# One mixed order for two attentions and twenty input tiles in a one-core decoder step

## The chip, the core and the metric

The kernel runs on one core of one Trainium2 chip. The metric is the device time of one execution, in microseconds (us). Its engines are TensorE (PE: matmuls and transposes), VectorE (DVE), ScalarE (ACT), GpSimd (POOL) and SyncE (SP, which here issues most DMAs). Each engine works through its own instructions in the order in which the program lists them; semaphores tie the engines together.

## The reference, cut to what matters

One decoder layer for a prompt group (512 tokens) and a sample group (8 sequences of 4 new tokens, each with 1024 cached positions in pages of 128). All is float32.

```python
z = rmsnorm(x, norm_mix_w) @ w_in        # 1024 -> gb, gc, u (512 each) and q, k, v (4 heads x 128)
yconv = gb * causal_dwconv(gc * u)        # conv mixer, width 3
s  = (q[c] . k[c]) * 64**-0.5 + rel_bias  # two score maps per head, c = 0, 1
a  = softmax(s[0]) - lam * softmax(s[1])
o  = rmsnorm(a @ v) * subln_w * 0.8       # per head; samples read k, v of 8 pages and the new ones
x += concat[yconv, o] @ w_out
x += cross_attention(rmsnorm(x), memory)  # 4 heads, 256 memory tokens
x += conv_ffn(rmsnorm(x))                 # 1024 -> 2 x 2816 -> 1024
```

## The kernel before

**Tiles.** Activations lie transposed, channels on the partitions, 544 columns: two halves of 256 prompt and 16 sample tokens. A projection is cut into tiles of 128 output channels. Each fp32 product is made from three fp32r ones: a weight tile `w_raw` is split into `w_hi` (`split_hi`, ACT, L1221) and `w_lo` (`split_lo`, DVE, L1518), and an activation into `a_hi` and `a_lo`. `tile(n)` (L936) does, for each of 8 blocks of 128 rows, w_hi by a_hi, w_hi by a_lo and w_lo by a_hi on both halves: 48 matmuls of 272 columns into the two banks of `proj[n % 2]`. DVE then takes the 544 columns out (`tile` on DVE, L1647, L1666), scaled by `rstd`. Tiles alternate between `proj[0]` and `proj[1]`.

**Order.** `make_schedule()` writes one list of steps. Each engine's program walks that list and emits its own part of a step, so the list is the order on every engine. The part that matters begins after the q tiles. Twenty tiles are left of the input projection: k0 to k3, v0 to v3, then gb, gc, u for each of four channel groups. Twelve of them each stand whole ahead of a portion of the samples' attention (`plan`). The other eight are spread in halves (`half_tile`, then `tile`) over the prompt's attention (`ticks`).

**Samples.** For each of two groups of four sequences and each pair of pages: `k_turn` transposes 8 pages' keys head by head through the banks T0 (copied out by ACT) and T1 (copied out by DVE), and `k_score` multiplies them with `q_rows` into S0. `s_soft` is a softmax over 1056 positions (DVE maximum, ACT exp, DVE scale). `s_turn` transposes the probabilities, `s_pv` (L1053) multiplies them with pages of values into S1, `s_new` adds the new tokens, `s_norm` normalizes (ACT squares, two table loads, scaled copies), `s_out` transposes into `b_hi` and `b_lo`. SP loads the pages, 8 at a time, into a ring of 16 (`load_self`); its eight register loads come before each group's eight DMAs.

**Prompt.** Sixteen units (four query blocks i by four heads h); unit u = 4i + h sees i + 1 key blocks. `p_score`: matmuls into S0 and S1 (L1079); DVE adds the bias (L1776, L1780) and takes the maximum (L1785); ACT takes exp, which frees S0 and S1 (L1382). `p_mix`: DVE forms p0/z0 - lam p1/z1 (L1799 to L1803). `p_turn`: transposes through T0, ACT copies to `p_keys` (L1390). `p_pv` (L1098): with the values into T1, 128 columns a head. After four heads `p_norm` (ACT, L1396 and the tables of L1226 and L1227), `p_scale` (DVE, T1 to `o_blk`), `p_out` (transposes, then ACT `b_hi`, DVE `b_lo`). A tick u of the old order is `p_mix(u-1)`, `p_out`, `p_score(u)`, `p_scale`, a half tile, `p_turn(u-1)`, `p_pv(u-2)`, `p_norm`.

**Mixer.** `conv(c)` (DVE, L1674 to L1535) follows the u tile; `mix(c)` (DVE, L1688 to L1690) multiplies with the gate and writes `b_hi` and `b_lo`.

The stage ends with the first tile of the output projection (`out add 0`), which needs all of `b_hi` and `b_lo`.

Of the kernel before, what the change touches and what calls it, by code (L numbers as in the profile page):

```python
# [17 lines left out]
F32 = mybir.dt.float32  # L18
# [6 lines left out]
P = 128  # L25
# [15 lines left out]
DIST = 384  # L41
# [55 lines left out]
def make_tiles():  # L97
# [36 lines left out]

def make_schedule():
# [18 lines left out]

    fill = [("in", "k", h) for h in range(HEADS)] + [("in", "v", h) for h in range(HEADS)]
    fill += [("in", kind, c) for c in range(CT) for kind in ("gb", "gc", "u")]
    after = {("in", "k", h): [("k_out", h)] for h in range(HEADS)}
    after |= {("in", "v", h): [("v_out", h)] for h in range(HEADS)}

    def turns(g, kq, hp, behind=None):  # L160


        steps = []
        for j in range(2):
            steps.append(("k_turn", g, kq, hp, j))
            if behind:
                steps.append(("k_score", g, *behind, j))
        return steps

    def keys(g, kq):  # L170
        return turns(g, kq, 0, (kq - 1, 1) if kq else None) + turns(g, kq, 1, (kq, 0))

    def scores(g, kq, hp):
        return [("k_score", g, kq, hp, j) for j in range(2)]


    plan = [keys(0, kq) for kq in range(4)]
    plan.append(scores(0, 3, 1) + turns(1, 0, 0) + turns(1, 0, 1) + [("s_soft", 0)])
    plan.append([("s_turn", 0)] + scores(1, 0, 0) + [("s_pv", 0, 0)])
    plan.append([("s_pv", 0, 1)] + keys(1, 1))  # L180
    plan.append([("s_pv", 0, 2)] + keys(1, 2))
    plan.append([("s_pv", 0, 3), ("s_new", 0)] + keys(1, 3) + [("s_norm", 0)])
    plan.append(scores(1, 3, 1) + [("s_soft", 1)])
    plan.append([("s_turn", 1), ("s_pv", 1, 0), ("s_pv", 1, 1)])
    plan.append([("s_pv", 1, 2), ("s_out", 0), ("s_pv", 1, 3), ("s_new", 1), ("s_norm", 1)])
    units = [(i, h) for i in range(SEQ // P) for h in range(HEADS)]

    half_at, fill_at = range(3, 17, 2), range(4, 18, 2)
    ticks = []
    for u in range(len(units) + 4):  # L190
        tick = []
        if 0 <= u - 1 < len(units):
            tick.append(("p_mix", *units[u - 1]))
        if u >= 4 and units[u - 4][1] == HEADS - 1:
            tick.append(("p_out", units[u - 4][0]))
        if u < len(units):
            tick.append(("p_score", *units[u]))
        if 3 <= u < len(units) + 3 and units[u - 3][1] == HEADS - 1:
            tick.append(("p_scale", units[u - 3][0]))
        if u in half_at:  # L200
            tick.append("half")
        if u in fill_at:
            tick.append("fill")
        if 0 <= u - 1 < len(units):
            tick.append(("p_turn", *units[u - 1]))
        if 0 <= u - 2 < len(units):
            tick.append(("p_pv", *units[u - 2]))
            if units[u - 2][1] == HEADS - 1:
                tick.append(("p_norm", units[u - 2][0]))
        ticks += tick  # L210
    assert len(plan) + len(fill_at) + 1 == len(fill)
    late = []
    for part in plan:
        f = fill.pop(0)
        tile(*f)
        if f[1] == "u":
            part = part + [("conv", f[2]), ("mix", f[2])]
        if ("s_new", 0) in part:
            part = late + part
        else:  # L220
            at = len(part) - 1 if part[-1][0] == "k_score" else 0
            part = part[:at] + late + part[at:]
        late = list(after.get(f, []))
        s.extend(part)
    ticks.insert(0, "fill")
    for n, step in enumerate(ticks):
        if n == 3:
            s.append(("s_out", 1))
        if step == ("p_pv", 3, 3):
            s.append(("mem_in",))  # L230
        if step == ("p_out", 3):
            s += [("half_tile", TILE["out", "add", 0]), step]
            s += [("squares", k, "mem") for k in range(KT)]
            continue
        if step == "half":
            s.append(("half_tile", TILE[fill[0]]))
            continue
        if step == "fill":
            f = fill.pop(0)
            tile(*f)  # L240
            if f[1] == "u":
                late += [("conv", f[2]), ("mix", f[2])]
            continue
        s.append(step)
        if step[0] == "p_score":
            s.extend(late[:1])
            late = late[1:]
        if step == ("p_turn", 3, 3):
            s.extend(late)
# [82 lines left out]

def number_fills():

    count = dict(S0=0, S1=0, T0=0, T1=0)
    out, held = [], {}

    def use(slot):
# [3 lines left out]
    for step in SCHEDULE:  # L342
        kind = step[0]
        uses = [use(slot) for slot in FILLS.get(kind, [])]
        if kind == "k_score":
            if step[3:] == (0, 0):
                held["k"] = use("S0")
# [1580 lines left out]
```

## Time and profile before

| what | value |
| --- | --- |
| median of 3 runs | 1054.36 us (1051.03 to 1056.3) |
| span of the profiled execution | 1050.4 us |
| TensorE busy | 973.8 us, 93% of the span |
| VectorE busy, ScalarE busy | 573.0 us (55%), 388.4 us (37%) |
| mean granted TensorE clock | 0.974 |
| the twenty tiles and both attentions, to the end of `out add 0` | 49.0 to 345.3 us, 296.3 us |

The profiled execution is one execution with its own time: for it the record has the span, from its first to its last instruction. That lies 4.0 us (0.4%) below the median of the three timed runs and 0.6 us below the lowest of them. Durations below are those of this one execution. A step can be found in the trace by its line. In the timelines the end of a matmul is modelled and overlaps the next one, so the time that a group takes is read from its start to the start of the next. An fp32 matmul with a separate moving operand (L1025, L1053, L1079, L1098) stands in the trace as two records; a transpose (L948) and an fp32r matmul (L936) as one.

### The profile page before, as it was taken

To read this page: it belongs to the slowest core of one execution; us is meant where nothing else is said; L and a number is where in the kernel's file an instruction comes from. 1 tells how busy PE (TensorE), PEld (TensorE's weight loads), DVE (VectorE), ACT (ScalarE), POOL (GpSimd) and SP (SyncE) were. 2 spreads that over 40 slices of the span, in tenths; PEclk is the share of its full clock that TensorE was granted. 3 is DMA by queue.
4 is the path that set the end of the run, shared out by engine and by line. 5 is a ranking of instruction groups with operands and counts; after the bars stand their busy time and mean duration, and the time that the engine had idled before them with its cause. 6 is when DMAs were issued, how large, how long until landed. Compare 5 with 4: busy or idle time off the path is not lost.

```text
span 1050.4 us, 19193 instructions
## 1 busy us (share of the span) xinstructions
PE 973.8 (93%) x7675; PEld 887.6 (85%) x7675; DVE 573.0 (55%) x997; ACT 388.4 (37%) x691; POOL 97.9 (9%) x213
## 2 busy tenths in 40 slices
PE   5999989977887999999888999999999999999995
PEld 5977766746777999998755999999999999999994
DVE  4544423627687646335433447778347783477542
ACT  5422212234436547224422335433124331243343
POOL 2211000000000011100000002222002220122000
PEclk8999998998999999999989999999999999999998
DMA  8656678831101245634562322323323223332213
GB/s 251 194 173 218 202 248 279 270 121 41 41 21 41 83 124 154 229 118 141 190 251 80 95 81 82 100 81 90 92 81 100 82 84 91 88 97 80 71 37 100
DMA packets 162492, 131.36 MB, mean 125 GB/s; under 512 B 5820, under 2 KB 139223, under 8 KB 162371
## 3 DMA queue, kind: packets, MB, share of 16 engines
q1 hardware_dynamic: 159940, 124.40, 38.4%
q0 software_dynamic: 2320, 5.68, 1.8%
q8 instruction: 61, 1.00, 0.4%
q14 instruction: 27, 0.21, 0.1%
q10 hardware_dynamic: 144, 0.07, 0.0%
HBM read 123.12 MB, written 7.00 MB: 124 GB/s over the span
## 4 chain that ended last, share of the span: by engine, by line
PE 78%; DVE 8%; ACT 6%; issue 4%; SPq 2%; DMA 2%; DVEq 0%; ACTq 0%
PE proj L936 63%; PE T L948 7%; PE score L1025 2%; PE score L1141 1%; PE score L1126 1%; PE score L1053 1%; ACT pages L1382 1%; DVE small L1785 1%; ACT w_hi L1221 1%; DVE score L1780 1%; DMA w_raw<-in_w_in 1%; SPq L659 1%; PE score L1159 1%; SPq L676 1%; DVE a_lo L1584 1%
## 5 line engine op out<-in xcount | busy, mean ns | idle before, releaser
L936 PE MATMUL proj<-a_hi,w_hi 128*128 128x272 f32 (+1 forms) x992 | 222.7, 296 | 4.8 <-DVE a_lo L1584 2.7
L936 PE MATMUL proj<-a_hi,w_lo 128*128 128x272 f32 (+1 forms) x992 | 216.9, 290 | 0.0
L936 PE MATMUL proj<-a_lo,w_hi 128*128 128x272 f32 (+1 forms) x992 | 216.8, 290 | 0.0
L1221 ACT ACTIVATE w_hi<-w_raw 128x1024 fp32r<-128x1024 f32 (+1 forms) x132 | 137.0, 1038 | 155.6 <-PE proj L936 144.6
L1518 DVE TENSOR_TENSOR w_lo<-w_raw,w_hi 128x1024 fp32r<-128x1024 f32 (+1 forms) x132 | 159.0, 1205 | 61.1 <-ACT w_hi L1221 60.7
L936 PEld LDWEIGHTS proj<-a_hi,w_hi 128*128 128x128 f32 x992 | 162.2, 191 | 16.1 <-issue 13.4
L936 PEld LDWEIGHTS proj<-a_lo,w_hi 128*128 128x128 f32 x992 | 162.5, 192 | 0.1
L936 PEld LDWEIGHTS proj<-a_hi,w_lo 128*128 128x128 f32 x992 | 161.5, 192 | 0.0
L936 PE MATMUL proj<-d_hi,w_hi 128*128 128x272 f32 x704 | 145.5, 288 | 0.0
L936 PE MATMUL proj<-d_hi,w_lo 128*128 128x272 f32 x704 | 144.8, 288 | 0.0
L936 PE MATMUL proj<-d_lo,w_hi 128*128 128x272 f32 x704 | 144.6, 287 | 0.0
L936 PEld LDWEIGHTS proj<-d_lo,w_hi 128*128 128x128 f32 x704 | 110.0, 188 | 0.0
L936 PEld LDWEIGHTS proj<-d_hi,w_hi 128*128 128x128 f32 x704 | 109.7, 188 | 0.2
L936 PEld LDWEIGHTS proj<-d_hi,w_lo 128*128 128x128 f32 x704 | 109.6, 189 | 0.0
L1625 DVE TENSOR_TENSOR x<-proj,x 128x544 f32<-128x544 f32 x40 | 29.0, 724 | 109.6 <-PE proj L936 109.6
L1474 ACT ACTIVATE conv<-up_pad,fvec 128x512 f32<-128x512 f32 x44 | 36.0, 818 | 134.8 <-DVE up_pad_s L1658 134.8
L890 POOL COPY f_state<-up_pad 128x2 f32<-128x2 f32 x44 | 47.4, 1077 | 306.6 <-DVE up_pad_s L1658 306.6
L1656 DVE TENSOR_TENSOR up_pad<-proj,rstd 128x512 f32<-128x512 f32 x44 | 30.4, 691 | 55.1 <-PE proj L936 47.8
L948 PE MATMUL T<-ident,pages 128*128 128x128 f32 x248 | 40.8, 304 | 13.4 <-DMA pages<-in_x_prompt 5.7
L948 PEld LDWEIGHTS T<-ident,pages 128*128 128x128 f32 x248 | 30.5, 154 | 26.3 <-issue 9.8
L1348 ACT ACTIVATE turned<-T 128x512 f32<-128x512 f32 x32 | 19.1, 597 | 79.0 <-PE T L948 79.0
L1703 DVE COPY turned<-T 128x512 f32<-128x512 f32 x32 | 22.1, 691 | 33.3 <-PE T L948 32.8
(257 smaller groups left out, 1262.9 us busy)
## 6 DMA issues: line engine op xcount, KB each, us to landing
w_raw<-in_w_up SPq DMA_DIRECT2D x44, 512.0 KB, 3.8
w_raw<-in_w_in SPq DMA_DIRECT2D x24, 512.0 KB, 4.8
pages<-in_cache_k SPq DMA_DIRECT2D x40, 256.0 KB, 4.4
early_pages<-in_cache_v SPq DMA_DIRECT2D x40, 256.0 KB, 4.7
w_raw<-in_w_ckv SPq DMA_DIRECT2D x16, 512.0 KB, 4.0
c_pages<-in_cache_mem_k SPq DMA_DIRECT2D x16, 512.0 KB, 6.4
c_pages<-in_cache_mem_v SPq DMA_DIRECT2D x16, 512.0 KB, 5.3
w_raw<-in_w_down SPq DMA_DIRECT2D x16, 448.0 KB, 3.7
```

Source lines behind the costliest of these rows:

```text
L659: physical.append(sp.value_load(page_ids[0:1, slot:slot + 1], min_val=0, max_val=src.shape[1] - 1))
L890: pool.tensor_copy(f_state[:, j * FT + i, 0:2], up_pad[:, j, i % 2, SEQ:SEQ + 2]).then_inc(sem("f_state_ready"), 1)
L936: mm = pe.matmul(proj[n % 2][:, half, 0:width], wt, act[:, k, half * HALF:half * HALF + width], start=(k == 0 and a == 0), stop=(k == w["k ...
L948: mm = pe.transpose(bank[use[0]][0:width, col:col + rows], src, ident[0:rows, 0:rows])
L1025: mm = pe.matmul(bank["S0"][32 * b:32 * b + 32, 0:2 * P], q_rows[:, h, GB * g + b, :], k_turned[:, half % 2, b, h2 * 2 * P:(h2 + 1) * 2 * ...
L1221: act.activation(w_hi[:, n % W_HI_RING, 0:kt, :], w_raw[:, n % W_RING, 0:kt, :], ACT.Copy).then_inc(w_hi_ready, 1)
L1348: act.activation(k_turned[:, half % 2, 2 * step[4], :], bank["T0"], ACT.Copy).then_inc(free["T0"], 1)
L1474: act.activation(prompt(conv[:, j, :]), by_half(up_pad[:, j, i % 2, 0:SEQ]), ACT.Identity, bias=bias, scale=w0).then_inc(sem("first_tap"), 1)
L1518: dve.tensor_tensor(w_lo[:, n % W_RING, 0:kt, :], w_raw[:, n % W_RING, 0:kt, :], w_hi[:, n % W_HI_RING, 0:kt, :].bitcast(F32), ALU.subtrac ...
L1625: dve.tensor_tensor(halves(x[:, w["i"], :]), out[:, :, 0:HALF], halves(x[:, w["i"], :]), ALU.add).then_inc(tile_out[arg % 2], 1)
L1656: dve.tensor_tensor(by_half(up_pad[:, j, i % 2, 2:2 + SEQ]), prompt_of(out), prompt(rstd), ALU.mult).then_inc(sem("up_in"), 1)
L1703: dve.tensor_copy(k_turned[:, half % 2, 2 * step[4] + 1, :], bank["T1"]).then_inc(free["T1"], 1)
```

## The change

The two attentions no longer follow one another. `mixed_periods()` makes twenty periods, one for each tile. In each, the samples' own events and up to two prompt ticks (`TICKS`) are merged in proportion, and the tile is cut into 16 pieces of three matmuls (first half 0, all 8 blocks, then half 1), which are dealt out between the events. All twenty tiles use `proj[0]` alone; each half is evicted by DVE by itself (`half_out`). The two banks of `proj[1]` become `N` (samples' scores) and `H` (samples' values). A prompt unit's `p_pv` uses T1 alone, and ACT copies it to `o_blocks` and squares it at once. `k_turn` handles one head of four sequences; the exp of a unit is a step of its own (`p_exp`); `p_scale` now stands ahead of `p_mix` and `p_score` in its tick. `split(n + 2)` stands at the head of period n. The order of the mixer's tiles becomes gc, u, gb, `conv` is cut in three parts that stand in the gb period, and `mix` at the head of the next.

```diff
-        for j, kind in enumerate(("gb", "gc", "u")):
+        for j, kind in ((1, "gc"), (2, "u"), (0, "gb")):
...
+AFTER_FILL = {("in", "k", h): [("k_out", h)] for h in range(HEADS)}
+AFTER_FILL |= {("in", "v", h): [("v_out", h)] for h in range(HEADS)}
+AFTER_FILL |= {("in", "gb", c): [("mix", c)] for c in range(CT)}
+TICKS = {7: [0], 8: [1], 9: [2, 3], 10: [4, 5], 11: [6, 7], 12: [8], 13: [9, 10], 14: [11], 15: [12], 16: [13],
+         17: [14], 18: [15], 19: [16]}
+def prompt_events(u):
...
+    first = [("p_scale", (u - 3) // HEADS)] if ends(u - 3) else []
+    if 0 <= u - 1 < PROMPT_UNITS:
+        first.append(("p_mix", *unit(u - 1)))
+    if u < PROMPT_UNITS:
+        first.append(("p_score", *unit(u)))
+    events = [first]
+    if u < PROMPT_UNITS:
+        events.append([("p_exp", *unit(u))])
+    if ends(u - 3) and (u - 3) // HEADS >= 2:
+        events.append([("p_out", (u - 3) // HEADS)])
+    if 0 <= u - 2 < PROMPT_UNITS:
+        events.append([("p_pv", *unit(u - 2))])
+    if 0 <= u - 1 < PROMPT_UNITS:
+        events.append([("p_turn", *unit(u - 1))])
+    if ends(u - 2):
+        events.append([("p_norm", (u - 2) // HEADS)])
...
+    samples.append(values(1, 3) + [[("s_new", 1)], [("p_out", 0)], [("s_out", 0)]])
+    samples.append(norm(1)[:3] + [[("p_out", 1)]] + norm(1)[3:])
+    samples.append([[("s_out", 1)]])
+    samples.append([])
...
+    for fill, events in zip(FILL_TILES, mixed_periods()):
+        n = TILE[fill]
+        s.append(("split", n + 2))
+        s += AFTER_FILL.get(FILL_TILES[FILL_TILES.index(fill) - 1], []) if n > FIRST_FILL else []
+        for j, event in enumerate(events):
+            for piece in range(PIECES * j // len(events), PIECES * (j + 1) // len(events)):
+                s.append(("piece", n, piece))
+                if piece == KT - 1:
+                    s.append(("half_out", n))
+                if piece == PIECES - 1:
+                    tile(*fill)
+            s += event
+    s += AFTER_FILL[FILL_TILES[-1]]
+    s.append(("mem_in",))
+    s += prompt_tick(PROMPT_UNITS + 1)
+    s.append(("half_tile", TILE["out", "add", 0]))
+    s += prompt_tick(PROMPT_UNITS + 2)
...
-                if (kind == "k_turn" and step[3:] == (0, 0)) or kind == "s_pv":
+                if (kind == "k_turn" and step[3] == HEADS - 1) or (kind == "s_pv" and step[3] == 1):
                     if self_loads:
                         load_self(*self_loads.pop(0))
...
+            def piece(n, part):
+                half, k = divmod(part, KT)
...
+                if k == 0 and n > FIRST_FILL:
+                    pe.wait_ge(half_out, 2 * (n - 1 - FIRST_FILL) + half + 1)
...
+                pe.matmul(out, w_h, a_hi[:, k, cols], start=(k == 0), stop=False)
+                pe.matmul(out, w_h, a_lo[:, k, cols], start=False, stop=False)
+                mm = pe.matmul(out, w_l, a_hi[:, k, cols], start=False, stop=(k == KT - 1))
+                if k == KT - 1:
+                    mm.then_inc(half_done if half == 0 else tile_done, 1)
...
+                elif kind == "p_pv":
+                    h = step[2]
+                    cols = slice(h * P, (h + 1) * P)
+                    wait_full(act, uses[0])
+                    o = o_blocks[step[1]][:, cols]
+                    act.activation(o, bank["T1"][:, 0:P], ACT.Copy).then_inc(free["T1"], 1)
+                    wait_taken(act, *uses[0])
+                    act.activation(o_sq[:, :], o, ACT.Square,
+                                   accum_out=small[:, 28 + h:29 + h]).then_inc(sem("o_squared"), 1)
```

## Rows read from the trace of the kernel before

**Rows 1.** Stretches of the span: busy us (instructions) per engine, granted clock, DMA share, GB/s.

```profile
49.00:101.70 52.70, 51.18 (x449) 41.63 (x448) 23.43 (x33) 14.45 (x24) 6.68 (x20) 1.00 0.59 187
...
227.50:345.30 117.80, 95.01 (x638) 82.92 (x638) 88.05 (x202) 56.67 (x155) 0.00 (x0) 0.91 0.13 37
49.00:345.30 296.30, 262.09 (x1997) 208.93 (x1997) 158.94 (x324) 103.63 (x243) 10.63 (x26) 0.95 0.47 149
```

**Rows 2.** TensorE's waits from 49 to 345.3 us: total us, times, longest.

```profile
PE score L1079 <- ACT pages L1382: 10.6, 8, 3.1
PE T L1098 <- DVE pages L1790: 4.8, 3, 3.4
...
PE T L948 <- DMA pages<-in_cache_k: 1.9, 1, 1.9
```

**Rows 3.** TensorE timeline, keys after a tile: start, us, instruction.

```profile
94.31 1.04 PE L948 MATMUL T<-ident,pages 128*128 128x128 f32 x8
95.28 0.64 PE L1025 MATMUL score<-turned,q_rows 128*32 128x256 f32 x8
95.85 1.09 PE L948 MATMUL T<-ident,pages 128*128 128x128 f32 x8
```

**Rows 4.** TensorE timeline, values of pages and one prompt unit.

```profile
134.36 1.92 PE L1053 MATMUL score<-early_pages,norm_area 128*32 128x512 f32 x16
...
299.06 0.49 PE L948 MATMUL T<-ident,pages 128*128 128x128 f32 x3
299.38 0.83 PE L1098 MATMUL T<-v_tok,pages 128*128 128x128 f32 x6
302.27 2.40 PE L1079 MATMUL score<-k_t,q_t 64*128 64x256 f32 x8 [2.05 <-ACT pages L1382]
```

**Rows 5.** Windows on a whole tile and two half tiles: busy us, granted clock.

```profile
88.20:94.31 6.11, 6.11 (x52) 6.11 (x49) 1.35 (x2) 0.75 (x1) 1.32 (x2) 1.00 0.93 289
...
304.60:308.66 4.06, 4.06 (x25) 4.06 (x25) 3.92 (x9) 0.00 (x0) 0.00 (x0) 0.74 0.00 0
...
312.48:315.59 3.11, 3.11 (x26) 3.11 (x25) 3.08 (x5) 3.06 (x7) 0.00 (x0) 1.00 0.02 5
```

**Rows 6.** VectorE timeline: mix, split, eviction, then p_mix and p_score of a unit.

```profile
301.32 0.71 DVE L1688 TENSOR_TENSOR norm_area<-norm_area 128x544 f32<-128x544 f32 x1
...
302.55 0.72 DVE L1690 TENSOR_TENSOR b_lo<-norm_area,b_hi 128x544 fp32r<-128x544 f32 x1
303.86 1.23 DVE L1518 TENSOR_TENSOR w_lo<-w_raw,w_hi 128x1024 fp32r<-128x1024 f32 x1 [0.59 <-ACT w_hi L1221]
305.00 0.72 DVE L1647 TENSOR_TENSOR norm_area<-proj,rstd 128x544 f32<-128x544 f32 x1
305.64 0.15 DVE L1799 RECIPROCAL small<-small 128x2 f32<-128x2 f32 x1
...
307.21 0.75 DVE L1776 TENSOR_SCALAR score<-score,near 128x512 f32<-128x512 f32 x1
...
308.66 1.22 DVE L1785 TENSOR_REDUCE small<-score 128x2 f32<-128x1024 f32 x1
```

**Rows 7.** ScalarE timeline: p_exp, p_turn, then the two table loads of p_norm.

```profile
309.92 0.69 ACT L1382 ACTIVATE pages<-score,small 128x512 f32<-128x512 f32 x1 [5.71 <-DVE small L1785]
...
311.26 0.59 ACT L1390 ACTIVATE pages<-T 128x512 f32<-128x512 f32 x1
...
312.90 1.28 ACT L1226 ACT_TABLE_LOAD   x1
...
315.81 0.20 ACT L1227 ACTIVATE small<-small 128x4 f32<-128x4 f32 x1
```

**Rows 8.** VectorE group from 227.5 to 345.3 us: busy, mean ns, idle before.

```profile
L1518 DVE TENSOR_TENSOR w_lo<-w_raw,w_hi 128x1024 fp32r<-128x1024 f32 x9 | 11.0, 1223 | 10.4 <-ACT w_hi L1221 10.4
```

**Rows 9.** VectorE timeline, first and last operation of one conv step.

```profile
293.48 0.68 DVE L1674 TENSOR_TENSOR pre<-pre,rstd 128x512 f32<-128x512 f32 x1
...
297.07 0.24 DVE L1535 SCALAR_TENSOR_TENSOR norm_area<-pre_s,vec,norm_area 128x32 f32<-128x32 f32 x1
```

More of the change, by code:

```diff
@@ new lines @@
+TICKS = {7: [0], 8: [1], 9: [2, 3], 10: [4, 5], 11: [6, 7], 12: [8], 13: [9, 10], 14: [11], 15: [12], 16: [13],
+         17: [14], 18: [15], 19: [16]}
+def prompt_events(u):
+    unit = lambda n: divmod(n, HEADS)
+    ends = lambda n: 0 <= n < PROMPT_UNITS and n % HEADS == HEADS - 1
+    first = [("p_scale", (u - 3) // HEADS)] if ends(u - 3) else []
[14 more added lines that the diff above has]
+        events.append([("p_norm", (u - 2) // HEADS)])
+    return [e for e in events if e]
@@ L153, in make_schedule @@
     s += [("near",), ("q_blocks",)]
[L155 to L249, printed above, removed]
+    for fill, events in zip(FILL_TILES, mixed_periods()):
[10 more added lines that the diff above has]
+            s += event
@@ L359, in number_fills @@
             uses = [held["s", step[1]]]
-        if kind == "p_pv":
-            if step[2] == 0:
-                held["p", step[1]] = use("T1")
-            uses = [held["p", step[1]]]
-        if kind in ("p_norm", "p_scale"):
-            uses = [held["p", step[1]]]
         if kind == "ck_score":
@@ L388 @@
 PAGE_GROUPS = [(step[1], "k" if step[0] == "k_turn" else "v", step[2]) for step in SCHEDULE
-               if (step[0] == "k_turn" and step[3:] == (0, 0)) or step[0] == "s_pv"]
+               if (step[0] == "k_turn" and step[3] == 0) or (step[0] == "s_pv" and step[3] == 0)]
 def self_page(g, cache, kq, b, pg):
@@ L632, in build @@
         LATE_NORMS = ["mem"]
+        AFTER_IN = TILE["out", "add", 0]
         use_of = {step: uses for step, uses, _ in NUMBERED}
@@ L1013, in _ @@
                         turn(uses[j], parts)
                 elif kind == "k_score":
[L1015 to L1016 removed]
+                    g, kq, h = step[1:]
+                    if h == 0:
                         pe.wait_ge(sem("q_rows_ready"), 2 * HEADS)
                         wait_empty(pe, uses[0])
[L1019 to L1022 removed]
@@ L1042, in _ @@
                 elif kind == "s_pv":
[L1043 to L1044 removed]
+                    g, kq, pg = step[1:]
+                    if kq == 0 and pg == 0:
                         wait_empty(pe, uses[0])
```

404 lines of the change are left out of this document (239 added, 165 removed), and 2 rows, old and new, of the table FILLS.

## The prediction

> **What bounds the kernel now.** I read the stretches of the span first. The change lies between 49.0 us (start of tile k0) and 345.3 us (end of `out add 0`), 296.3 us; what comes before and after is not touched. In that stage TensorE is busy for 262.1 us and idle for 34.2, at a mean granted clock of 0.95. The first stretch is dense (51.2 busy of 52.7, clock 1.00); the last, where the prompt's attention runs, is not (95.0 of 117.8, clock 0.91, VectorE busy for 88.1) [rows 1]. The list of waits says for whom: 10.6 us of p_score for the exp that frees S0 and S1, 4.8 us of p_pv for p_scale, 1.9 us in one wait for late pages [rows 2].
>
> How much of the stage is TensorE's own work? A tile takes 6.11 us and there are twenty and `out add 0`: 128. Eight transposes of a k_turn take 0.97 (94.31 to 95.28), a k_score 0.57 (95.28 to 95.85), 32 of each: 49 [rows 3]. The values of one group of pages take 1.92, eight of them 15 [rows 4]. A prompt unit with three key blocks takes 0.32 for p_turn and 0.83 for p_pv [rows 4], and about 0.9 for the scores, an estimate, since the one shown ran partly at the low clock; over sixteen units with one to four blocks that is 26. The other transposes (k_out, v_out, s_turn, p_out, mem_in and the rest) are some 130 at 0.12: 16, with s_new 2. Sum 236. So before, waits and slow clock hold 60 us, and that is all that a new order can give back. If the pieces hid every one, the time would fall by 5.7%. The question is how many it puts in their place.
>
> **What the order adds on TensorE.** A whole tile behind a k_score took 6.11 and a half tile 3.11 [rows 5]. Two equations, 48m + r and 24m + r, give m = 0.125 a matmul and r = 0.11 for the return from small matmuls to the tile. There are 80 events with small matmuls (32 k_score, 16 s_pv, 16 p_score, 16 p_pv), each now followed by a piece; before some 28 such returns: 52 x 0.11 = 6. Three matmuls in succession into one bank instead of two banks in turn: not in these rows; bounds 0 and, if every one of 960 cost 0.01 more, 10. I take 0, as it is the same number of columns.
>
> **What it removes.** Late pages: a period with keys is 13 to 15 us and one with values about 10, and a page group is now asked for at the last read of its slots, two groups ahead; I count the wait of 1.9 us as gone. Waits of the samples' steps for copies mostly go, since a piece of 0.375 us stands between.
>
> **What it adds: a split at the head of each period.** `split(n + 2)` stands ahead of everything else of a period: ACT 1.05 [rows 7], then DVE 1.23 [rows 6], so DVE is free 2.3 us into the period at the earliest, and 0.7 later has copied k_out or v_out out of T0. The first k_turn is ready for T0 after k_out (0.64) and two pieces (0.75): it waits 1.05 us in four periods, 1.4 in that of gc0, and about 2 more go to s_turn and T1 in two others. Queued behind are all pieces. Waits of the first ten periods: 7; they come to 130 us.
>
> **The chain through DVE and ACT.** For a unit with four key blocks p_mix is 1.6 us (305.64 to 307.21) and p_score 2.7 (307.21 to 309.88) on DVE [rows 6], then exp 1.4 on ACT (309.92 to 311.3) [rows 7]; for one block I take 1.1, 0.9 and 0.8. A conv is 3.8 (293.48 to 297.31) [rows 9], a mix 1.95 (301.32 to 303.27), two half evictions 0.44 each (one of all columns is 0.72 [rows 6]; bounds 0.36 and 0.72). p_norm on ACT is 3.1 (312.90 to 316.01) [rows 7]. DVE already stood for 10.4 us ahead of nine splits, waiting for ACT's half [rows 8]. I followed the new list step by step from period 10 (gb0), counting from each period's start:
> - gb0 has 19 events for 16 pieces. DVE: split, copy, conv, mix, score of unit 4 to 9.9, and so on to 14.8. TensorE waits 2.3; 16.9 long.
> - gc1: ACT has p_norm(0) ahead of its split, so w_hi comes at 3.4, w_lo at 4.6, then mix 6.5, scores of samples 7.2, p_scale 7.9, p_mix(5) 9.1. p_turn(5) was ready at 6.7. Waits 2.9; 17.0 long.
> - u1: s_turn's third fill of T0 waits for DVE, which has the split, p_mix(7) and p_score(8) first (5.9): 3.3 of waits; 12.4 long.
> - gb1: conv on DVE ahead of unit 8's mix; then p_norm(1) runs on ACT from 14.4 to 17.5, and p_scale(1) now stands ahead of p_mix(9) and p_score(10) on DVE. p_turn(9), ready at 16.3, goes at 19.7. Waits 7.7; 20.0 long.
> - gc2 and u2: what DVE is late holds back the eviction of a half: 2.2; 22.6 long.
> - gb2: p_out(0) fills T0; `b_hi` stands behind exp(13) on ACT, `b_lo` behind p_score(13) and its exp: T0 is free at 14.25 and p_turn(12) was ready at 10.0. 4.3; 16.6 long.
> - gc3: p_norm(2) delays the split to 5.0; mix, p_scale: p_out(2) goes at 7.7 instead of 4.0. Then p_out(1) needs T0, whose `b_hi` stands behind exp(14) (13.3) and s_norm's tables (16.4) on ACT: from 9.0 to 17.9 TensorE stands. 12.7; 21.9 long.
> - u3 and gb3: 3.1, the last p_turn behind the conv; 19.1 long.
> - Behind the last period: mem_in, p_pv(15), p_norm, p_scale, p_out, `out add 0`: 12.9 with 3.5 of waits.
>
> Waits of these: 42; with the first ten 49. A dip of the clock has cost a half tile 0.95 us (4.06 for 3.11, at a mean of 0.74 [rows 5]); four of the waits are over 3 us, so 4.
>
> **Sum.** 236 + 6 + 49 + 4 = 295 us for a stage of 296.3: the span goes from 1050.4 to 1049, and the median of the runs, 4.0 above the profiled execution, from 1054.4 to 1053. The waits of which the kernel is rid and those that it gets are about equal. The two orders have the same weakness, 3.1 us of tables ahead of a split or an exp; the new one adds p_scale ahead of p_score and three p_out behind them.
>
> ScalarE's tables decide much of this, and here row and skill differ. Each load took 1.28 and the next instruction began 0.02 later [rows 7]. The Trainium skill (ScalarE: Activation LUTs, "What ACT_TABLE_LOAD costs") gives 1283 ns for the load too, and about 1380 ns of drain with it, 2.66 us in all. By the page a p_norm would be 5.8 us, and six norms would give up to 16 us more, a time of 1069; by the row it is 3.1. I go by the row.
>
> **Rivals.**
> (A) The forecast: 1053, of itself 1043 to 1064. Chance 0.40.
> (B) The pieces hide more: every late step of DVE starts the next ones late too, and I may have counted one delay in two periods; also where TensorE runs ahead, later waits shrink. If half of the 49 us go, and two dips with them, the stage is 268: 1026. For it speaks that DVE needs only 159 of 296 us in the stage [rows 1]; against it, that the waits are for order and not for throughput, as the 10.4 us ahead of the splits show. Chance 0.30.
> (C) Slower, by the clock. TensorE works some 93 of 127 us in the eight periods gb0 to gc3, with stands of 1 to 9 us all through, where the last stretch before has a clock of 0.91 [rows 1]. At a mean of 0.75 the 93 us become 124, at 0.91 they are 102: 22 more, a time of 1075. It decides from about 0.86 on (108, 6 more). Against it: the first ten periods have short stands alone, and the first stretch before, with such, has 1.00 [rows 1]. The Trainium skill (TensorE: Matmul & The Clock Gate, "A second HAM failure mode: psum-queue depth-cycling") tells of a kernel whose many small idles between groups of matmuls made the clock swing; by it the dense ten periods would suffer as well. Chance 0.20.
> (D) Pages late. A group and a tile's weights are 2.6 MB in a period; the periods with values are 10 us, 260 GB/s, where the first stretch moved 187 at a share of 0.59 [rows 1]. Two us in each of six periods: 1065. Against it, twice the rate is not needed for long. Chance 0.10.
>
> **How the numbers follow.** About 0.5% (5.3 us) is what a measurement of this kernel can tell from no change. A lies under 1049.1 with a third of its chance, over 1059.6 with a tenth: 0.13, 0.23, 0.04. B is faster but for 0.01; C slower, 0.20; D half same and half slower. Faster 0.42, same 0.29, slower 0.29. The range is 1019 to 1075: it takes in B with 7 us below its time, since the share of the waits that goes may be more than half, and ends at C's; about 0.08 is left below and 0.10 above. The bounds of the unknown costs (return 0 to 0.11 each, bank 0 to 10, eviction 0.36 to 0.72, which is 0 to 6 over the periods in which DVE is late) lie inside.
>
> **What would show it.** Right: in gc3 TensorE stands for about 9 us ahead of the transposes of p_out(1), released by DVE's `b_lo`; in gb1 about 3.4 ahead of p_turn(9), DVE idle ahead of p_scale for some 5 us; in gb2 some 4 ahead of p_turn(12); about 1 ahead of the first k_turn in k1 to k3; no wait for pages over 1 us. The ten first periods end near 179 us, the stage near 344. Wrong: a stage under 280 with these stands short (B); a clock under 0.86 from gb0 to gc3 (C); waits of L948 or L1053 for DMA (D). What I may have mis-sized is above all the propagation of lateness between the three queues, as every entry above hangs on the one before it.

## The result and the profile after

| | us |
|---|---|
| kernel before, median of 4 runs | 1053.6 (1051.0 to 1056.3) |
| kernel after, median of 4 runs | 1064.7 (1063.7 to 1066.0) |
| ratio after / before | 1.011, 95% interval 1.009 to 1.013 |
| predicted | 1053.0, range 1019 to 1075 |

Forecast was no change; the kernel is 1.1% slower. The page of the profile after begins so (span; then busy time, share of the span and instructions of each engine):

```profile
span 1063.1 us, 19216 instructions
PE 975.9 (92%) x7675; PEld 891.3 (84%) x7675; DVE 575.2 (54%) x1021; ACT 394.9 (37%) x707; POOL 98.0 (9%) x213
```

The stage runs from 49.06 to 355.78 us, 306.7 long where before had 296.3 [rows 1]: 10.4 of the span's 12.7 us. The rest of the difference (2.2 us) lies behind the stage, where nothing was changed; in the profiles of the fifteen kernels below, none of which touches that part, it took 703.5 to 707.5 us, in part by how much low clock it had. So a difference of 2 to 4 us between two profiled executions can lie there. The stretches of after, in the columns of [rows 1]:

```profile
49.06:355.78 306.72, 262.96 (x1996) 211.70 (x1995) 160.55 (x347) 109.90 (x259) 10.62 (x26) 0.93 0.45 143
49.06:101.00 51.94, 46.09 (x390) 38.00 (x389) 21.23 (x33) 13.40 (x21) 8.00 (x22) 0.97 0.54 166
...
297.95:321.08 23.13, 12.70 (x77) 11.66 (x77) 10.15 (x19) 11.63 (x28) 0.00 (x0) 0.69 0.08 23
305.30:318.95 13.65, 5.57 (x27) 5.28 (x26) 5.80 (x11) 5.91 (x11) 0.00 (x0) 0.50 0.00 0
56.15:59.55 3.40, 3.40 (x20) 2.70 (x13) 0.44 (x1) 0.00 (x0) 0.00 (x0) 0.50 0.00 0
...
250.70:257.55 6.85, 6.58 (x28) 5.63 (x27) 2.43 (x7) 4.19 (x10) 0.00 (x0) 0.50 0.22 82
...
188.16:321.08 132.92, 106.50 (x725) 82.51 (x723) 79.40 (x184) 55.69 (x146) 0.00 (x0) 0.87 0.35 110
```

Such rows split a stage in three. TensorE's idle time is length less busy. Low clock is the stretches at 0.50, the lower of the two levels (1.2 GHz); half of the busy time in them is counted as lost against the full clock, which is an estimate. What is left is work at the full clock. After has nine such stretches in the stage, three of which stand above, with 44.6 us and 35.4 busy; before has five, with 27.5 and 23.9 (its stage ends 0.2 us earlier here than in [rows 1]).

| stage, us | length | idle | lost to low clock | work at full clock |
|---|---|---|---|---|
| before | 296.1 | 34.2 | 12.0 | 249.9 |
| after | 306.7 | 43.8 | 17.7 | 245.2 |
| predicted for after | 295 | 49 | 4 | 242 |

So the mixed order did save 4.7 us of work, and paid 9.6 of idle time and 5.7 of clock. TensorE's waits, called stands below, in the stage (total, times, longest), where [rows 2] were those of before:

```profile
PE T L991 <- DVE b_lo L1831: 11.2, 2, 8.1
PE T L991 <- DVE p_exp L1867: 4.8, 4, 2.5
PE T L991 <- DVE turned L1855: 4.0, 2, 2.3
PE T L991 <- DVE norm_area L1801: 3.8, 2, 3.3
PE T L991 <- ACT o_blk L1441: 3.5, 1, 3.5
PE T L991 <- DVE v_tok L1762: 3.4, 2, 2.7
PE T L991 <- DVE norm_area L1759: 3.3, 3, 1.1
PE proj L1066 <- POOL q_rows L853: 2.1, 1, 2.1
```

The 10.6 us for S0 and S1 have become 1.5 and the wait for pages is gone. In their place nearly every wait is one of a transpose (L991) for a bank or an operand: a short instruction of VectorE or ScalarE that stands behind another step in its queue. The timeline shows three places.

```profile
65.81 1.23 DVE L1563 TENSOR_TENSOR w_lo<-w_raw,w_hi 128x1024 fp32r<-128x1024 f32 x1 [0.71 <-ACT w_hi L1258]
...
66.95 0.69 DVE L1759 COPY norm_area<-T 128x512 f32<-128x512 f32 x1
...
67.78 1.06 PE L991 MATMUL T<-ident,pages 128*128 128x128 f32 x8 [1.11 <-DVE norm_area L1759]
...
194.05 0.60 PE L991 MATMUL T<-ident,early_pages 128*128 128x128 f32 x4
198.19 0.66 PE L991 MATMUL T<-ident,early_pages 128*128 128x128 f32 x4 [3.54 <-ACT o_blk L1441]
...
196.95 0.47 ACT L1427 ACTIVATE p_exp<-score,small 128x256 f32<-128x256 f32 x1 [6.35 <-DVE small L1850]
...
309.16 0.69 ACT L1427 ACTIVATE p_exp<-score,small 128x512 f32<-128x512 f32 x1 [6.55 <-DVE small L1850]
...
310.62 1.28 ACT L1263 ACT_TABLE_LOAD   x1
...
312.23 1.28 ACT L1264 ACT_TABLE_LOAD   x1
...
313.63 0.67 ACT L1420 ACTIVATE b_hi<-T,sub_w 128x512 fp32r<-128x512 f32 x1
...
314.40 0.75 DVE L1831 SCALAR_TENSOR_TENSOR b_lo<-T,sub_w,b_hi 128x512 fp32r<-128x512 f32 x1 [4.87 <-ACT b_hi L1420]
...
315.30 1.09 PE L991 MATMUL T<-ident,turned 128*128 128x128 f32 x4 [8.08 <-DVE b_lo L1831]
```

First, k1: `split` ahead of the copy of k_out; TensorE stands for 1.11 us. Second, gb0: k_turn needs T1, which holds p_pv(2), whose copy is behind exp(4) on ScalarE, which waited for VectorE's maximum. Third, gc3: p_out(2) has filled T0; its `b_hi` on ScalarE is behind exp(14) and the two table loads of the samples' norm; p_out(1) stands for 8.1 us, from 307.2 to 315.3, and a low clock of 13.65 us lies around it: it begins at 305.3, 1.9 us ahead of the stand and behind an earlier one of 2.3 us, and ends 3.7 us behind it.

### The profile page after: what moved, and what is told of

Read it like the earlier page. It is cut to its first block, busy times and chain, and to the rows that moved or that the text cites. A ratio compares the mean times of both kernels' runs of the same rounds, so it can differ in the third digit from the quotient of the medians.

```text
span 1063.1 us, 19216 instructions
## 1 busy us (share of the span) xinstructions
PE 975.9 (92%) x7675; PEld 891.3 (84%) x7675; DVE 575.2 (54%) x1021; ACT 394.9 (37%) x707; POOL 98.0 (9%) x213
## 4 chain that ended last, share of the span: by engine, by line
PE 76%; DVE 9%; ACT 6%; issue 4%; SPq 2%; DMA 1%; POOL 0%; DVEq 0%; ACTq 0%; POOLq 0%
PE proj L961 56%; PE T L991 7%; PE proj L979 3%; PE proj L981 2%; PE proj L980 2%; PE score L1178 1%; ACT w_hi L1258 1%; DMA w_raw<-in_w_in 1%; PE proj L1066 1%; PE score L1163 1%; DVE w_lo L1563 1%; ACT p_exp L1427 1%; DVE small L1850 1%; SPq L681 1%; SPq L698 1%
## 5 line engine op out<-in xcount | busy, mean ns | idle before, releaser
L961 PE MATMUL proj<-a_hi,w_hi 128*128 128x272 f32 (+1 forms) x672 | 152.8, 294 | 4.7 <-DVE a_lo L1629 2.6
L961 PE MATMUL proj<-a_hi,w_lo 128*128 128x272 f32 (+1 forms) x672 | 150.0, 290 | 0.0
L961 PE MATMUL proj<-a_lo,w_hi 128*128 128x272 f32 (+1 forms) x672 | 149.8, 289 | 0.0
L961 PEld LDWEIGHTS proj<-a_hi,w_hi 128*128 128x128 f32 x672 | 111.6, 192 | 6.7 <-issue 4.4
L961 PEld LDWEIGHTS proj<-a_lo,w_hi 128*128 128x128 f32 x672 | 111.2, 191 | 0.1
L961 PEld LDWEIGHTS proj<-a_hi,w_lo 128*128 128x128 f32 x672 | 110.5, 191 | 0.0
L979 PE MATMUL proj<-a_hi,w_hi 128*128 128x272 f32 x320 | 108.1, 338 | 1.1 <-DVE norm_area L1691 1.1
L981 PE MATMUL proj<-a_hi,w_lo 128*128 128x272 f32 x320 | 95.3, 298 | 0.0
L980 PE MATMUL proj<-a_lo,w_hi 128*128 128x272 f32 x320 | 95.2, 298 | 0.0
L979 PEld LDWEIGHTS proj<-a_hi,w_hi 128*128 128x128 f32 x320 | 63.4, 198 | 29.1 <-issue 24.8
L980 PEld LDWEIGHTS proj<-a_lo,w_hi 128*128 128x128 f32 x320 | 63.8, 199 | 0.0
```

The source lines that it names most:

```text
L961: mm = pe.matmul(proj[n % 2][:, half, 0:width], wt, act[:, k, half * HALF:half * HALF + width], start=(k == 0 and a == 0), stop=(k == w["k ...
L979: pe.matmul(out, w_h, a_hi[:, k, cols], start=(k == 0), stop=False)
L980: pe.matmul(out, w_h, a_lo[:, k, cols], start=False, stop=False)
L981: mm = pe.matmul(out, w_l, a_hi[:, k, cols], start=False, stop=(k == KT - 1))
```

## The experiments

T1: the stands come from what lies ahead of short copies in the queues of VectorE and ScalarE, so moving a step regains them. T2: the cut into pieces costs by itself. T3: the stands bring the low clock, which about doubles what they cost. In each diff, minus is the kernel after, unless the text says otherwise. Ratios are to the kernel before, timed beside each kernel; the kernel after has 1.0111. The kernels were timed in groups, and the kernel before had medians from 1052.2 to 1054.1 us in them, so a difference of medians from two groups can be off by up to 2 us; 0.001 of the ratio is 1.05 us. How idle time and clock share a gain is read from one execution of each kernel.

### Two blocks of eight pieces

```diff
-            for piece in range(PIECES * j // len(events), PIECES * (j + 1) // len(events)):
+            block = {0: range(KT), len(events) // 2: range(KT, PIECES)}.get(j, ())
+            for piece in block:
```

> The kernel after, but each tile's sixteen pieces stand in two blocks of eight, one ahead of a period's first event and one at its middle; events, their order and all work are the same. Theory T1 (waits placed by the order on the queues of VectorE and ScalarE set the time, and the cut itself costs nothing): the events of a half period stand with no pieces between them, so their chains are bare again, 10 us or more slower than the kernel after (1075 or more). Theory T2 (the cut into three-matmul pieces, with its changes of bank and weights, costs): about 100 returns fewer, at 0.05 to 0.1 us each 5 to 10 us faster (1055 to 1060). Theory T3 (the clock): the longer stands bring more low clock, another 5 us slower.

1057.7 us, ratio 1.0041 (1.0024 to 1.0058): 7 us faster than after. T1's number was wrong, and wrong in sign. The stretches say why (the stage, k1 to k3, gb3):

```profile
49.31:348.69 299.38, 256.47 (x1997) 208.96 (x1995) 160.13 (x347) 108.91 (x259) 10.62 (x26) 0.93 0.46 147
63.61:102.58 38.97, 38.97 (x355) 31.98 (x352) 17.60 (x27) 10.81 (x19) 3.98 (x6) 1.00 0.67 225
321.39:327.65 6.26, 6.26 (x53) 6.26 (x52) 3.09 (x10) 3.45 (x9) 0.00 (x0) 1.00 0.29 86
```

Work at the full clock is 241.4 us (256.5 less half of 30.2 busy at the low clock), 3.8 less than after: that is T2's part, measured. And k1 to k3 have no wait at all, as eight pieces, 3 us, cover the split. The idle time of the stage is hardly less all the same, 42.9 us for 43.8: gb1 stands for 5.5 us and not 2.4, v0 for 2.5 and not 1.0. In gb3 the sixteen pieces stand together and take 6.10 us from start to start, as much as the whole tile of before in two banks (6.11). So this run could not tell the cut from the split's place; a later one does (below).

### The split behind the second event

```diff
-        s.append(("split", n + 2))
...
             s += event
+            if j == min(1, len(events) - 1):
+                s.append(("split", n + 2))
```

> The kernel after, but the split of the tile after next stands behind the second event of a period, not ahead of all, on every engine that takes part. T1: the 1.1 us stands of TensorE in three keys periods and the 2.7 us in the period of the first gc tile (VectorE still in the split when its copy out of the bank is due) go: 4 to 6 us faster, 1059 to 1061. Rival: the split is then late for the tile that needs it or moves the same wait one event on: within 1.5 us of the kernel after.

1043.4 us, ratio 0.9914 (0.990 to 0.9928): 21 us faster than after and faster than before, by one step moved. It was put at 4 to 6. Stretches (stage, k1 to k3, gc3) and the longest waits:

```profile
49.18:336.17 286.99, 256.63 (x1996) 207.51 (x1995) 161.67 (x348) 109.39 (x259) 10.54 (x26) 0.95 0.49 153
65.69:105.67 39.98, 39.93 (x355) 32.47 (x352) 17.87 (x27) 10.82 (x18) 3.99 (x6) 1.00 0.70 216
...
283.23:303.21 19.98, 12.63 (x78) 11.81 (x77) 10.15 (x19) 11.64 (x28) 0.00 (x0) 0.71 0.09 26
```

```profile
PE T L992 <- DVE b_lo L1832: 9.3, 2, 7.4
PE T L992 <- ACT o_blk L1442: 4.0, 1, 4.0
```

The stands at the head of k1 to k3 are gone (0.05 us idle of 40). But they were 3.3 us. The profiled stage is 19.7 us shorter: 13.4 of idle time and 5.7 of low clock (23.9 us busy in it and not 35.4). By periods: gc0 3.9 us, gc1 3.5, gc3 3.1, u1 2.0, tail 1.8, gb2 1.4, gb1 1.1. The other periods change by less than 0.9 us. That the steps behind the split on both queues were late by its 2.3 us, anew at the head of a period, fits this; it was followed in the timeline for k1 alone.

### Output blocks 1 and 2 one and two periods later

```diff
-    if ends(u - 3) and (u - 3) // HEADS >= 2:
+    if ends(u - 3) and (u - 3) // HEADS >= 3:
...
-    samples.append(norm(1)[:3] + [[("p_out", 1)]] + norm(1)[3:])
-    samples.append([[("s_out", 1)]])
-    samples.append([])
+    samples.append(norm(1))
+    samples.append([[("s_out", 1)], [("p_out", 1)]])
+    samples.append([[("p_out", 2)]])
```

> The kernel after, but the prompt's output block 1 is transposed in the period of the last u tile and block 2 in that of the last gb tile, each one or two periods later than now; nothing else moves. T1: the 8.1 us stand ahead of block 1 and the 2.4 us ahead of block 2 in the last gc period go, 1 to 3 us of them come back in the last two periods: 6 to 9 us faster, 1056 to 1059. T3: 3 to 4 us of work at the low clock are regained too: 1053 to 1055. T2: the stands only covered other work, within 2 us of the kernel after (1063 to 1066).

1060.4 us, ratio 1.0064 (1.0044 to 1.0083), 4 us faster (5 by the ratios): between T1 and its rival. gc3 loses its stand (idle 1.9 us for 10.4), and u3, which had none, stands now, for the samples' norm on ScalarE:

```profile
PE T L991 <- ACT norm_area L1411: 4.8, 1, 4.8
PE proj L979 <- DVE norm_area L1691: 1.7, 1, 1.7
```

The second of these still counts to gc3. The 4.8 us are those of `s_out`, which reads what the norm writes. So moving p_out out of the way leaves a stand for whatever comes behind the samples' norm with its two table loads on ScalarE.

### Output block 1 ahead of the samples' norm, with the later split

```diff
-    samples.append(norm(1)[:3] + [[("p_out", 1)]] + norm(1)[3:])
+    samples.append([[("p_out", 1)]] + norm(1))
```

> The kernel with the split behind the second event of a period, and in it the transpose of output block 1 first in the last gc period, ahead of the samples' last row norm and not between its parts: the norm's part with the two table loads now stands behind the copies of output blocks 1 and 2 on ScalarE. T1: the 7.35 us stand ahead of block 1 goes but for 1 to 2 us, and 3 us of low clock behind it: 6 to 9 us faster than with the split alone, 1034 to 1037. Rival (the output blocks' move in the period of the last u tile only exchanged one stand for another): the norm is then late for the samples' output transposes in the next period, a new stand of 3 to 5 us there, 1040 to 1043.

1037.1 us, ratio 0.9852 (0.9834 to 0.987): 6.3 faster than with the split alone, as T1 had it. gc3 went from 20.0 us to 13.5, and the stand that the rival expected in u3 is 0.2 us.

### Product with the values ahead of the exponential

```diff
     events = [first]
+    if 0 <= u - 2 < PROMPT_UNITS:
+        events.append([("p_pv", *unit(u - 2))])
     if u < PROMPT_UNITS:
         events.append([("p_exp", *unit(u))])
...
-    if 0 <= u - 2 < PROMPT_UNITS:
-        events.append([("p_pv", *unit(u - 2))])
```

> The kernel after, but in each prompt unit the product with the values (of the unit two back) stands ahead of the exponential of this unit, not behind it. T1: the copy of that product out of bank T1, on ScalarE, no longer stands behind the exponential, which waits for VectorE's maximum; the 3.5 us stand in the period of the first gb tile goes, and 1 to 2 us in the other periods: 3 to 6 us faster, 1059 to 1062. Rival: ScalarE now starts the exponential later, the chain of the unit is longer and the turn of its probabilities waits: 0 to 5 us slower.

> As the last, and the product with the values ahead of the exponential in each prompt unit. T1 by the run of that edit alone (8 us off the kernel after, 3.5 us of which was the stand in the period of the first gb tile): 3 to 7 us faster than without it, 1029 to 1033. Rival: the probabilities' turns wait instead, 0 to 2 us.

On the kernel after: 1056.1 us, ratio 1.0023 (1.0007 to 1.0038), 8.6 faster (9.3 by the ratios); but the stand in gb0 did not go. The transpose there now stood 3.1 us for another copy of ScalarE behind the same exp (`turned`, L1388). In the profiled execution the stage is 7.4 us shorter: 2.3 us of idle time, and 4.8 of clock, as 9.7 us less of busy time lie at the low clock. With split and block 1 moved: 1040.9 us, ratio 0.9895 (0.9878 to 0.9913), 3.8 slower than without the edit, outside of both expectations; its gb0 and gb2 are together 3.8 us shorter, its gc3 4.0 longer. Its stage:

```profile
49.48:329.83 280.35, 251.34 (x1996) 203.42 (x1995) 160.37 (x347) 109.25 (x259) 10.52 (x26) 0.98 0.50 157
```

This is 1.6 us shorter than the stage of the kernel without the edit (282.0, below), with 3.1 us more of idle time and 5.3 less lost to the clock; the part behind the stage is 2.2 us longer. So this profile does not show the 3.8 us of the timed runs. The edit moves stands from one bank and period to another; why it costs time here is open.

### Exponential last

```diff
-    if u < PROMPT_UNITS:
-        events.append([("p_exp", *unit(u))])
...
         events.append([("p_turn", *unit(u - 1))])
+    if u < PROMPT_UNITS:
+        events.append([("p_exp", *unit(u))])
```

> The kernel with the later split and block 1 first, and in each prompt unit the exponential behind the product with the values and the turn of the unit before, not ahead of them, on every engine. T1: ScalarE's copies out of T0 and T1 no longer stand behind an exponential that waits for VectorE's maximum; the 4.0 us stand in the period of the first gb tile goes and 2 us in each of gb2 and gc3: 4 to 8 us faster, 1029 to 1033. Rival: the next unit's scores then wait for the banks that the late exponential frees, in the periods with two units or three: 2 to 6 us slower, 1039 to 1043.

1035.0 us, ratio 0.9814 (0.9797 to 0.9831), on top of split and block 1: 2.1 us by the medians, 4.0 by the ratios, whose intervals do not meet. It is at the low end of T1. The wait for `o_blk` is gone from the trace, gb0 is 3.0 us shorter (20.5 to 17.4), gc3 1.4 longer.

### The table loads left out

```diff
-                done(act.activation(out, in_, ACT.Ln, bias=eps[0:out.shape[0], 0:1], scale=width_scale))
+                done(act.activation(out, in_, ACT.Identity, bias=eps[0:out.shape[0], 0:1], scale=width_scale))
```

> The kernel after with the logarithm in the six 1/sqrt of the attention's row norms left out (a linear function stands in its place, so those rows' scale is another): ScalarE then loads no table there, 12 loads of 1.283 us less, all else the same. T1 (ScalarE's and VectorE's queues carry the waits): 2.6 us off the 8.1 us stand ahead of output block 1, 2.6 us off the tail, some off the rest, 4 to 8 us faster than the kernel after (1057 to 1061), and with the low clock that goes with the stands up to 12. Rival: the loads lie in time that ScalarE has over, within 2 us (1063 to 1066).

> The kernel before with the same logarithm left out in the same six places, 12 loads of 1.283 us less. If the table loads cost both orders the same, the difference to the kernel before is that of the change's kernel to the one without the logarithm; my theory is that the mixed order, with its whole stage waiting on two queues, pays more: before gains 1 to 4 us (1049 to 1052), the kernel after 4 to 8.

After: 1051.0 us (10 runs, 1047.3 to 1058.3), ratio 0.9992 (0.9973 to 1.0011), 12 to 14 us less. Before: 1046.9, ratio 0.9945 (0.9924 to 0.9965), 5 to 6 less. The same 15.4 us of ScalarE cost the mixed order more than twice what they cost the old one, and both more than expected. The profiled execution of the first was one of its longer ones (span 1055.5), so its rows are not used for the split of the gain; in it the stand ahead of output block 1 is 6.2 us and not 8.1.

### 48 matmuls that feed nothing, in the longest stand

```diff
                 elif kind == "p_out":
+                    if arg == 1:
+                        wait_taken(pe, *use_of["k_score", 1, 3, HEADS - 1][0])
+                        n = TILE["in", "gc", 3]
+                        for _ in range(48):
+                            pe.matmul(bank["N"][:, 0:HALF], w_hi[:, n % W_HI_RING, KT - 1, :], a_hi[:, 0, 0:HALF],
+                                      start=True, stop=True)
```

> The kernel after with 48 matmuls more, of a piece's shape, 6.0 us of them at the full clock, into a bank that nothing reads any more, issued ahead of the transpose of output block 1, where TensorE stands for 8.1 us. They feed nothing. T3 (it is the stand that brings the low clock behind it): the 13.7 us of low clock from 305.3 us on go or shrink to 3.4, and the kernel is 3 to 6 us faster with 6 us more of work, 1058 to 1062. Rival (the low clock comes anyway, or follows the load and not the stands): no change or slower, 1064 to 1067.

1061.3 us, ratio 1.006 (1.0045 to 1.0076): 3.4 us faster (5.4 by the ratios) with 6.0 us more of work. The stage, and gc3:

```profile
49.60:356.85 307.25, 270.22 (x2045) 219.42 (x2044) 161.86 (x348) 109.87 (x259) 10.63 (x26) 0.93 0.45 143
298.97:320.36 21.39, 17.64 (x125) 16.70 (x125) 10.15 (x19) 11.62 (x28) 0.00 (x0) 0.91 0.08 25
```

TensorE is busy for 17.6 us and not 12.7, the stand of 8.1 us is 1.3, the clock 0.91 and not 0.69 (one low stretch of 3.4 us for one of 13.65), and the period is 1.7 us shorter. VectorE and ScalarE do the same in the same time (10.15 and 11.6 busy). The 3.4 us that are left begin, as before, ahead of the stand; what is gone is the rest, 10.2 us. So at this place, in these two executions, the longer low clock came with the stand and not with the load. T3 is not shown for the stage or the time: the stage is 0.5 us longer (307.25 for 306.72), with a new low stretch of 6.3 us at its end, and all of the profiled execution's gain lies behind it, in a part that is 3.6 us shorter. Where the 3.4 us of the timed runs come from is open.

### Two blocks again, now with the split out of the way

> The kernel with the later split and output block 1 first in the last gc period, and its pieces in two blocks of eight for each tile. T2 (the cut costs work): by the run with coarse pieces TensorE's work at the full clock falls by 3.8 us, so 2 to 4 us faster than the same with fine pieces (1033 to 1035). T1 (the pieces cover the chains of VectorE and ScalarE, once the split is out of their way): waits of the events grow by more than that, 3 to 10 us slower (1040 to 1047).

1053.0 us, ratio 0.9992 (0.998 to 1.0004), against 0.9852 with fine pieces: 15 us slower by the ratios, 16 by the medians. Stage of this one, then of the one with fine pieces:

```profile
49.22:343.04 293.82, 256.66 (x1996) 209.89 (x1995) 160.00 (x347) 108.30 (x259) 9.69 (x26) 0.94 0.47 150
```

```profile
49.56:331.55 281.99, 256.07 (x1996) 207.42 (x1995) 161.12 (x348) 108.95 (x259) 10.72 (x26) 0.96 0.50 156
```

Busy time is equal, but of the coarse one 31.3 us are at the low clock, of the fine one 22.8: work 241.0 and 244.7. The cut costs 3.7 us, as in the first run, and saves 11.2 of idle time (37.2 and 25.9) and 4.2 of clock. So T2 is real, and small.

### Split in the middle of a period

Minus is here the kernel with the later split and block 1 first.

```diff
-            if j == min(1, len(events) - 1):
+            if j == len(events) // 2 - 1 or len(events) == 1:
```

> The kernel with the later split and block 1 first, but the split in the middle of a period and not behind its second event. If what counts is alone that the split is behind the copies of the period's head: the same as behind the second event, 1035 to 1039. If every place costs what stands behind it: one stand exchanged for another, up to 4 us slower. If the samples' and the prompt's chains at the head of a period all profit: 1 to 4 us faster, above all in the period of the first gb tile.

1036.7 us, ratio 0.9829 (0.9806 to 0.9852), beside 1037.1 and 0.9852 (0.9834 to 0.987): not told apart. Here it is enough that the split stands behind the copies of the period's head; with the other repairs in place it is not (next experiment).

### Nine pieces ahead in k0, and all repairs together

```diff
-            for piece in range(PIECES * j // len(events), PIECES * (j + 1) // len(events)):
+            deal = lambda e: PIECES * e // len(events) if n > FIRST_FILL or not 0 < e < len(events) else 8 + 8 * e // len(events)
+            for piece in range(deal(j), deal(j + 1)):
```

> The kernel after, but in the period of k0 nine of the sixteen pieces stand ahead of the first event and the rest go one or two to an event. T1: the 2.05 us stand for GpSimd's q_rows is covered, and with it the 3.4 us of low clock behind it: 2 to 4 us faster than the kernel after, 1061 to 1063. Rival: the seven events with one piece each between them bring new waits for the copies of T0 and T1, within 1 us (1064 to 1065).

> Later split, output block 1 first, exponential last, and the pieces of k0 ahead. If repairs add: the run with the exponential last less 2 to 4 us for k0, 1031 to 1033. If lateness only moves on: 1034 to 1036.

> The same with the split in the middle of a period. By the run with the split in the middle alone (0.4 us less, inside its interval) no difference to the split behind the second event, 1031 to 1033; if the chain of the period with the second norm's table loads profits, 1029 to 1031.

Alone on the kernel after: 1061.5 us, ratio 1.0076 (1.0063 to 1.009), 3 us faster, with an interval that just meets that of the kernel after (1.009 to 1.0132); k0 takes 13.2 us and not 16.6, at a clock of 1.00. All together, with the split behind the second event, 1030.7 us, ratio 0.9782 (0.9768 to 0.9795); with the split in the middle 1026.6 us, ratio 0.9739 (0.9726 to 0.9753), 4 us less again, better than expected, and the two intervals do not meet. So the place of the split within a period does count once the other stands are gone; in the profiles u1 is 2.7 us shorter, gb0 and gc3 1.1 each, gb1 4.1 longer. These repairs added up; the values ahead of the exponential did not. The stage and the longest waits of the last:

```profile
49.48:320.53 271.05, 250.47 (x1996) 201.75 (x1995) 161.08 (x347) 108.52 (x259) 9.70 (x26) 0.98 0.52 162
```

```profile
PE T L993 <- DVE p_exp L1869: 5.2, 3, 2.7
PE proj L1094 <- ACT norm_area L1413: 2.9, 1, 2.9
```

This is the mixed order with four moves of steps, 2.6% faster than the kernel before and 3.7% faster than the kernel after. Idle 20.6 us, lost to clock 4.8, work 245.7, in an execution that was the longest of five (1029.8 us).

## Why the prediction was wrong

**The step that failed** is the term "4 clock dips" of the sum 236 + 6 + 49 + 4. It measured 17.7 us, 14 more, and that alone carries the stage from 295 past its 306.7. I priced one dip of 0.95 us for each of the four stands over 3 us; there were nine stretches at the low clock, of up to 13.65 us, and two of them (56.15, 161.95) came behind stands of 2.1 and 2.7 us in the ten periods that I had taken for clean. The row for the price [rows 5] was one mild case. The trace of before has worse ones:

```profile
144.00:165.60 21.60, 18.02 (x133) 12.16 (x131) 5.75 (x8) 3.25 (x7) 0.00 (x0) 0.84 0.80 270
231.60:241.85 10.25, 7.36 (x28) 6.00 (x29) 6.34 (x28) 3.45 (x19) 0.00 (x0) 0.50 0.00 0
```

The second lost 3.7 us by itself (half of 7.36). The first, where TensorE stands up to 1.9 us for pages, lies among the dense stretches, which I judged by the one with clock 1.00. The mean clock of 0.91 in [rows 1], which I used for a rival alone, was the better row: the periods gb0 to gc3 came at 0.87 with 106.5 us busy. Rival C named this (93 us of work at 0.86 are 108) and was given 0.20.

**As a difference to the kernel before, the 60 us failed too.** The prediction gave before 236 us of work and 60 of waits and clock; the table has 249.9 and 46.2. So it had work going up by 6 and waits and clock down by 7, where work went down by 4.7 and waits and clock up by 15.3. The 242 us of work for after came near the 245.2 measured only because the work fell, which was not forecast, from a value that the 236 had put 14 us too low. With before's measured work the same terms give 309 us. What makes TensorE's work less in the mixed order is not shown.

**The other terms.** Waits 49, measured 43.8, by errors that cancel: 7 and 10.8 in the first ten periods, 42 and 33 behind them. For the returns I counted 80, before 28, at 0.11 us each. In the traces TensorE comes back from small matmuls to a tile 134 times in after, 28 in before and 40 in the kernel with two blocks, and the 94 returns between the last and after cost 3.8 us: 0.04 each. Matmuls of one bank in succession cost nothing that shows.

**Period by period**, with the waits forecast and measured: k1 to k3 1.05 each, 1.11; gc0 1.4, 2.7; gc1 2.9, 1.8; u1 3.3, 3.3; gb2 4.3, 3.5; gc3 12.7, 10.4, with about 9 ahead of p_out(1), 8.1; the tail 3.5, about 6. The stand in gc3 has the place and the releaser forecast, and the page waits went as forecast. Missed: k0's 2.1 us for GpSimd's `q_rows`, which a whole tile had hidden before and two pieces do not; and gb0's 3.5 us for T1 (4.0 in all, forecast 2.3). Too much: gb1 7.7, where p_turn(9) hardly stood (2.4 in all), gc2 with u2 2.2 for 1.1, and u3 with gb3 3.1 for none. The first ten periods ended at 188.2 us and not at 179: 3.8 us of the 9 are waits, 3.4 the two low stretches.

**What a new order can give back.** Measured, it is 46 us and not 60; the best order found makes the stage 25 us shorter (296.1 to 271.1). I took gains and losses to cancel, where the split at the head of a period was by itself worth 21 us. I had costed it at its first effect (about 1 us of TensorE in a period) and not at what stood behind it on two queues in the later periods.

**Rivals.** B (the pieces hide more) was not this kernel but is near the repaired one: 1026.6 us for 1026, with a stage of 271 for 268; that took four moves of steps, so the agreement is no merit of B. C was right in kind and at half its size: 11 us slower and not 22, at a clock of 0.87, just above the 0.86 that I had set as its sign. D (pages late) did not appear: the list of TensorE's waits in the stage has none for a DMA.

**Tables.** A load took 1.28 us and the next instruction began 0.02 later here too (310.62 to 311.92, where 1.28 of 1.30 is the load). The drain of the Trainium skill (ScalarE: Activation LUTs, "What ACT_TABLE_LOAD costs") is not seen in either kernel. Without the loads, 15.4 us of ScalarE, the mixed order gained 12 to 14 us and the old one 5 to 6, so what they cost depends on where they stand in the queue. The swinging clock that the Trainium skill tells of ("A second HAM failure mode: psum-queue depth-cycling", TensorE: Matmul & The Clock Gate) agrees with this trace in part: the clock did swing in the ten dense periods, but twice, each time behind one stand of over 2 us, and seven times behind them.

**Open.** Why the values ahead of the exponential help the kernel after and hurt the repaired one. Where the gain from the 48 matmuls that feed nothing lies. Why one stand is followed by the low clock and another of the same length is not (below).

## What to carry to other kernels

In this kernel, cutting a long block into pieces between short steps paid only once the short copies that free the banks came first in the queues of the other engines. So try first: put a long step that is due much later (a split for the tile after next, a norm with table loads) behind them, and no copy behind an instruction that waits for a third engine. The last is not safe by itself: of the two edits that did it, the exponential last gained 4 us by the ratios, the values ahead of it lost 4. Give idle time a price for the clock, as a range: in the seventeen profiles of this case the clock cost 0.15 to 0.6 us for each us of idle time (17.7 on 43.8 in the kernel after, 12.0 on 34.2 before, 3.4 on 23.0 in one of the repaired ones). Take it from the mean clock of the stretch most like the new one, not from the mildest dip. Before an order is judged, try where in the period the one step that all queues share should stand: here that was worth twice the change's whole loss.

## What was not expected of the hardware

The same stand need not bring the low clock. In k0, TensorE stood for 2.64 us for `q_rows` in the kernel with the later split and in the one with the values ahead as well; the first had a low stretch behind it, the other none:

```profile
49.18:65.69 16.51, 13.87 (x112) 11.68 (x110) 6.33 (x10) 3.34 (x5) 3.92 (x16) 0.90 0.19 56
```

```profile
49.48:64.43 14.95, 12.31 (x111) 10.51 (x110) 6.34 (x10) 3.34 (x5) 3.91 (x16) 1.00 0.22 60
```

That is 1.56 us for the same instructions. The kernels with block 1 first and with the exponential last make a second such pair: 3.0 us of idle time in k0 in both, 16.9 us at 0.90 in the one and 15.3 at 1.00 in the other. Runs of one kernel spread by more than that, 1051.3 to 1059.2 us in the twelve with the values ahead of the exponential. And idle time filled with matmuls that feed nothing made a period 1.7 us shorter, though not the stage.
